# Softmax denominators of differential attention: from ones-matmuls to running sums on VectorE and GpSimd

## What is computed

```
def differential_attention(q, k, v, lam, lambda_init, subln_g):
    # q,k: (B,S,H,2,64), H=4; v: (B,S,H,128)
    s = einsum('bqhcd,bkhcd->bhcqk', q, k) * scale - slope[h] * (qpos - kpos)
    s = where(kpos <= qpos, s, -inf)
    p = softmax(s, axis=-1)                # one for each of the two components c
    a = p[:, :, 0] - lam * p[:, :, 1]
    o = einsum('bhqk,bkhv->bqhv', a, v)
    return rmsnorm(o, subln_g) * (1 - lambda_init)
```

## Time and profile before

| | us |
|---|---|
| median of 3 runs | 2340.25 |
| the three runs | 2335.2, 2340.25, 2495.3 |
| the profiled execution | 2335.61 |
| span of its slowest core (core 4) | 2334.0 |
| spans of all cores | 2320.5 to 2334.0 |
| mean granted TensorE clock of the cores | 0.928 to 0.932 of full speed |

### The profile page before, as it was taken

How to read it: one execution, slowest core, us unless ns; L and a number is a source line. 1 busy time by engine, 2 the same in 40 slices (tenths; PEclk the granted TensorE clock), 3 DMA queues, 4 the chain that set the end, 5 groups by cost and what they waited for, 6 DMA issues and landing times.

```text
span 2334.0 us, 27831 instructions; the slowest of 8 cores (2320.5 to 2334.0 us)
## 1 busy us (share of the span) xinstructions
PE 1940.9 (83%) x9248; PEld 775.1 (33%) x9248; DVE 678.2 (29%) x797; ACT 1198.8 (51%) x1754; POOL 168.3 (7%) x265
## 2 busy tenths in 40 slices
PE   2378767779999999999999886698889449999999
PEld 1133323332232233232223221343333224444444
DVE  2245445540101101111111243444442131414131
ACT  2165444538888788887888774435421120303030
POOL 1100000000000000000000111111111000000000
PEclk9699889999999999999999998798899769999999
DMA  5477886610000002000100001120100641111101
GB/s 102 81 141 144 152 144 153 146 46 1 1 1 1 1 1 73 1 1 1 45 29 1 6 26 51 40 82 8 75 37 28 224 163 43 67 54 55 55 19 63
DMA packets 45738, 137.64 MB, mean 59 GB/s; under 512 B 6144, under 2 KB 11392, under 8 KB 45216
## 3 DMA queue, kind: packets, MB, share of 16 engines
q1 hardware_dynamic: 36528, 106.28, 14.0%
q0 software_dynamic: 9072, 29.59, 8.7%
HBM read 148.66 MB, written 43.12 MB: 82 GB/s over the span
## 4 chain that ended last, share of the span: by engine, by line
PE 59%; DMA 11%; DVE 9%; ACT 9%; issue 8%; POOL 3%; ACTq 0%; DVEq 0%; POOLq 0%; SPq 0%
PE psum L152 59%; DVE arena L152 9%; ACT arena L152 9%; DMA arena<-xkv 4%; DMA arena<-w_in 4%; POOL arena L152 3%; DMA arena<-w_b 3%; DMA arena<-x1s 1%; ACTq L142 0%; DVEq L142 0%; DMA arena<-cst 0%; DMA arena<-xhalo 0%; DMA arena<-biastab 0%; SPq L152 0%; POOLq L142 0%
## 5 line engine op out<-in xcount | busy, mean ns | idle before, releaser
L152 PE MATMUL psum<-arena 128*128 128x512 bf16 (+3 forms) x9248 | 1940.9, 373 | 389.2 <-DVE arena L152 163.9
L152 PEld LDWEIGHTS psum<-arena 128*128 128x128 bf16 (+1 forms) x9248 | 775.1, 100 | 1554.5 <-issue 935.4
L152 ACT ACTIVATE arena<-psum,arena 128x1024 bf16<-128x1024 f32 (+2 forms) x872 | 765.8, 901 | 220.2 <-PE psum L152 194.4
L152 ACT ACTIVATE arena<-psum 128x512 f32<-128x512 f32 (+2 forms) x352 | 193.2, 573 | 632.9 <-PE psum L152 592.0
L152 DVE COPY arena<-psum 128x1024 bf16<-128x1024 bf16 (+1 forms) x148 | 99.9, 684 | 707.5 <-PE psum L152 707.2
L152 ACT ACTIVATE arena<-arena 128x1 f32<-128x1 f32 (+3 forms) x397 | 203.8, 519 | 194.5 <-DMA arena<-x1s 88.1
L152 DVE SCALAR_TENSOR_TENSOR arena<-arena 128x1024 bf16<-128x1024 f32 (+3 forms) x150 | 164.6, 1098 | 383.0 <-ACT arena L152 349.5
L152 POOL TENSOR_TENSOR arena<-arena 128x128 bf16<-128x128 bf16 (+3 forms) x192 | 132.2, 691 | 1138.6 <-ACT arena L152 665.3
L152 DVE SCALAR_TENSOR_TENSOR arena<-psum,arena 128x512 bf16<-128x512 f32 x208 | 147.5, 713 | 177.1 <-ACT arena L152 163.7
L152 DVE TENSOR_TENSOR arena<-psum,arena 128x512 f32<-128x512 f32 x128 | 88.2, 691 | 324.8 <-PE psum L152 247.9
L152 DVE RECIPROCAL arena<-arena 128x512 f32<-128x512 f32 x32 | 107.0, 3344 | 0.0
(11 more groups left out here) (9 smaller groups left out, 3.8 us busy)
## 6 DMA issues: line engine op xcount, KB each, us to landing
arena<-xkv SPq DMA_DIRECT2D x80, 512.0 KB, 5.4
arena<-x1s SPq DMA_DIRECT2D x32, 512.0 KB, 3.4
arena<-w_b SPq DMA_DIRECT2D x16, 1024.0 KB, 7.5
w_b<-w POOLq DMA_DIRECT2D x8, 1024.0 KB, 12.9
w_b<-w POOLq DMA_DIRECT2D x16, 512.0 KB, 7.0
x1s<-arena SPq DMA_DIRECT2D x16, 512.0 KB, 2.6
out<-arena SPq DMA_DIRECT2D x16, 512.0 KB, 2.7
wg_b<-w_in POOLq DMA_DIRECT2D x4, 1024.0 KB, 12.9
```

Of the source, the lines that this page charges most:

```text
L152: return lambda e: getattr(e, name)(*a, **k)
```

## The change

The two ones-matmuls of each tile are taken out. In their place the probabilities of a tile are added, element by element, into a float32 buffer of 128 x 1024 (`accs`): component 0 by VectorE, component 1 by GpSimd, each 512 columns (fewer in diagonal tiles). The first tile of a pass is a copy in place of an addition. There are two such buffers, used by head passes in turn. Two tiles after the last one of a pass (`finalize_part1b`) a float32 matmul of ones for each component sums the buffer over partitions into banks 6 and 7. The reciprocals read these banks directly, so VectorE's two copies are gone, and the two multiplications with them move from VectorE to GpSimd. ScalarE's copies stay where they were (`finalize_part1a`). `finalize_part2` comes eight tiles after the last one in place of six. `NPT` goes from 4 to 8.

```diff
--- before.py
+++ after.py
@@ -492,7 +492,8 @@
         ONT_END = A2.get(0)
         o_bias = A2.get(NBC * 4)
         o_tri = A2.get(256); o_ones = A2.get(256); o_onesf = A2.get(512)
-        NPT = 4
+        NPT = 8
+        o_acc = [A2.get(4096) for _ in range(2)]
         o_PT = [A2.get(2048) for _ in range(NPT)]
         o_f = [A2.get(2048) for _ in range(7)]
         onT = view(o_onT, [4, 2048], BF16)
@@ -504,6 +505,8 @@
         t_bias = Tok("bias"); t_const2 = Tok("const2")
         t_PT = [Tok("PT") for _ in range(NPT)]
         t_f = [Tok("f") for _ in range(7)]
+        accs = [view(o, [1024], F32) for o in o_acc]
+        t_acc = [[Tok("acc") for _ in range(2)] for _ in range(2)]
         P.emit("sync", I("dma_start", out=biasv, in_=biastab), writes=[t_bias], stream="ld_c")
         P.emit("pool", I("dma_start", out=tri, in_=cst[:, 128:256]), writes=[t_const2], stream="ld_cp")
         P.emit("dve", I("memset", ones, 1.0), writes=[t_const2])
@@ -563,6 +566,11 @@
                 lst[-1]["last"] = True
                 tiles += lst
         NT = len(tiles)
+        _g = -1
+        for tl_ in tiles:
+            if tl_.get("first", False):
+                _g += 1
+            tl_["grp"] = _g
         ptc = [0]
         sc = [0]
 
@@ -609,24 +617,32 @@
             pt, c0 = tl["pt"], tl["c0"]
             first = tl.get("first", False)
             last = tl.get("last", False)
+            a_ = tl["grp"] % 2
             for comp in range(2):
                 rhs = PT[pt][:, 512 * comp + c0:512 * comp + 512]
                 P.emit("pe", I("matmul", bank(4 + comp)[:, c0:512], lhsT=Vp[pos][:, t, h * 128:(h + 1) * 128], rhs=rhs,
                                start=first, stop=last), reads=[t_V[pos], t_PT[pt]], writes=[tb[4 + comp]])
+            for comp, eng in ((0, "dve"), (1, "pool")):
+                src = PT[pt][:, 512 * comp + c0:512 * comp + 512]
+                dst = accs[a_][:, 512 * comp + c0:512 * comp + 512]
+                if first:
+                    P.emit(eng, I("tensor_copy", out=dst, in_=src), reads=[t_PT[pt]], writes=[t_acc[a_][comp]])
+                else:
+                    P.emit(eng, I("tensor_tensor", out=dst, in0=dst, in1=src, op=ALU.add),
+                           reads=[t_PT[pt]], writes=[t_acc[a_][comp]])
+
+        def finalize_part1a():
+            P.emit("act", I("activation", out=fo1, in_=bank(4), func=AF.Copy), reads=[tb[4]], writes=[t_f[0]])
+            P.emit("act", I("activation", out=ft2, in_=bank(5), func=AF.Copy), reads=[tb[5]], writes=[t_f[1]])
+
+        def finalize_part1b(a_):
             for comp in range(2):
-                rhs = PT[pt][:, 512 * comp + c0:512 * comp + 512]
-                P.emit("pe", I("matmul", bank(6 + comp)[:, c0:512], lhsT=ones, rhs=rhs,
-                               start=first, stop=last), reads=[t_const2, t_PT[pt]], writes=[tb[6 + comp]])
-
-        def finalize_part1():
-            P.emit("act", I("activation", out=fo1, in_=bank(4), func=AF.Copy), reads=[tb[4]], writes=[t_f[0]])
-            P.emit("dve", I("tensor_copy", out=fz1, in_=bank(6)), reads=[tb[6]], writes=[t_f[2]])
-            P.emit("act", I("activation", out=ft2, in_=bank(5), func=AF.Copy), reads=[tb[5]], writes=[t_f[1]])
-            P.emit("dve", I("tensor_copy", out=fz2, in_=bank(7)), reads=[tb[7]], writes=[t_f[3]])
-            P.emit("dve", I("reciprocal", out=fz1, in_=fz1), reads=[t_f[2]], writes=[t_f[2]])
-            P.emit("dve", I("tensor_tensor", out=fo1, in0=fo1, in1=fz1, op=ALU.mult), reads=[t_f[2]], writes=[t_f[0]])
-            P.emit("dve", I("reciprocal", out=fz2, in_=fz2), reads=[t_f[3]], writes=[t_f[3]])
-            P.emit("dve", I("tensor_tensor", out=ft2, in0=ft2, in1=fz2, op=ALU.mult), reads=[t_f[3]], writes=[t_f[1]])
+                P.emit("pe", I("matmul", bank(6 + comp), lhsT=onesf, rhs=accs[a_][:, 512 * comp:512 * comp + 512],
+                               start=True, stop=True), reads=[t_const2, t_acc[a_][comp]], writes=[tb[6 + comp]])
+            P.emit("dve", I("reciprocal", out=fz1, in_=bank(6)), reads=[tb[6]], writes=[t_f[2]])
+            P.emit("pool", I("tensor_tensor", out=fo1, in0=fo1, in1=fz1, op=ALU.mult), reads=[t_f[2]], writes=[t_f[0]])
+            P.emit("dve", I("reciprocal", out=fz2, in_=bank(7)), reads=[tb[7]], writes=[t_f[3]])
+            P.emit("pool", I("tensor_tensor", out=ft2, in0=ft2, in1=fz2, op=ALU.mult), reads=[t_f[3]], writes=[t_f[1]])
             P.emit("dve", I("scalar_tensor_tensor", out=fo, in0=ft2, scalar=small[:, 3:4], in1=fo1, op0=ALU.mult, op1=ALU.add),
                    reads=[t_f[0], t_f[1], t_small], writes=[t_f[4]])
             P.emit("pool", I("tensor_tensor", out=fsq, in0=fo, in1=fo, op=ALU.mult), reads=[t_f[4]], writes=[t_f[5]])
@@ -657,16 +673,24 @@
             tl = tiles[i]
             emit_pv(tl)
             if tl.get("last", False):
-                finalize_part1()
-                sched.append((i + FDELAY, tl["s"], tl["h"]))
+                finalize_part1a()
+                sched.append((i + 2, "b", tl["grp"] % 2, None))
+                sched.append((i + 2 + FDELAY, "2", tl["s"], tl["h"]))
+                sched.sort(key=lambda x: x[0])
                 if tl["h"] == 3 and tl["s"] > 0:
                     load_p3a_group(3 - tl["s"])
             while sched and sched[0][0] <= i:
-                _, s_, h_ = sched.pop(0)
-                finalize_part2(s_, h_)
+                _, kind_, a1_, a2_ = sched.pop(0)
+                if kind_ == "b":
+                    finalize_part1b(a1_)
+                else:
+                    finalize_part2(a1_, a2_)
         while sched:
-            _, s_, h_ = sched.pop(0)
-            finalize_part2(s_, h_)
+            _, kind_, a1_, a2_ = sched.pop(0)
+            if kind_ == "b":
+                finalize_part1b(a1_)
+            else:
+                finalize_part2(a1_, a2_)
 
         def alias(tok, olds):
             for o in olds:
@@ -676,7 +700,7 @@
                         tok.r[ins.stream] = ins
             return tok
 
-        P2_TMP = [t_bias, t_const2] + t_PT + t_f
+        P2_TMP = [t_bias, t_const2] + t_PT + t_f + t_acc[0] + t_acc[1]
         KV03 = kv_toks([0, 1, 2, 3])
         KV47 = kv_toks([4, 5, 6, 7])
         A3 = Alloc([(kvm(0), kvm(4)), (M47_FREE, kvm(8)), (KV_END, COMMON_END), (ONT_END, ARENA_BYTES)])
```

## The result

The changed kernel took 2610.52 us in the median of nine runs (2605.89 to 2696.54) against 2342.14 for the kernel before; the ratio of the two is 1.1147, with a 95% interval of 1.113 to 1.1164. It is slower by 268 us. The forecast was slower, 2558 us, in a range of 2420 to 2760.

A forecast was written before the change was run, and what follows sets the result against it. TensorE was taken to bound the attention, and after the change VectorE and GpSimd excluding each other; 202 - 10 + 26 = 218 us on 2335.6 gave 2554, or 2558 us against the median, range 2420 to 2760.

The forecast's parts named there:

- What bounds the kernel and what the removal is worth: Attention tiles: TensorE sets 1.29 us in heads 1 to 3; removing two matmuls saves at most 69 us.
- the faster rival: Full tiles: GpSimd repeats within 1.13 us, ScalarE sets the pace, 69 us saved, near 2271 us; chance 0.06.
- GpSimd's price: GpSimd's accumulation per tile: between 1.04 and 1.27 us, repeating alone every 1.21 to 1.44 us.
- The exclusion: Full tiles: VectorE and GpSimd accumulations exclude each other, so the period is their sum, 1.49 to 1.69, taken 1.59 us.
- the rival without overlap: Full tiles: the two accumulations exclude each other without start-up overlap, period 1.96 us, 2735 us in total; chance 0.14.
- The clock: Attention tiles: TensorE, 54% busy, gets a mean clock near 0.8, lengthening the period from 1.59 to 1.64 us.
- The end of a head: Diagonal tiles 8.0 us plus net finish 4.5 us: 12.5 us a head against 10.9 before.
- The buffers: End of a head: Exps run on until eight PT buffers are full, which spares nothing, GpSimd being late.
- The sum: Whole kernel: 202 us for full tiles, less 10 for head 0, plus 26 for ends of heads, 218 us more.

The follow-up runs named there:

- The PSUM run: Changed kernel with both accumulations kept, but VectorE's running sum in PSUM banks 6 and 7, copied to SBUF at the end of a head: 2473.43 us.
- the run with four: Changed kernel with four PT buffers in place of eight: 2650.01 us, ratio 1.1321.

## Why the prediction was right, point by point

**What bounds the kernel and what the removal is worth.** TensorE's six matmuls were the bound, as read. That removing them could give at most 69 us rested on 1.13 us as ScalarE's period. That was too long: in the kernels with one sum on VectorE, Exps recorded at 1.11 us follow one another every 1.08 us, and every 1.00 us where the scores lie ready. The step was mis-sized; it had no part in the sum, but it made the gain of the faster rival smaller than it would be.

**GpSimd's price.** Bounds 1.04 and 1.27; measured 1.15 alone. The repeat of 1.21 to 1.44 holds too: 1.30. The lower bound was no like of it, though: the row of 1038 ns is the square, which reads one tile twice. The products of the new finish, f32 into f32 from two tiles, take 1.26, so the type of the output isn't what sets the two prices apart. Why they differ stays open.

**The exclusion.** The reading of three overlaps carried the forecast, and it was right, also for plain tensor_tensor, which no row had shown. The parts were 0.93 to 1.13 and 0.56, sum 1.49 to 1.69, taken 1.59, the middle, which nothing decided. Measured 1.01 and 0.55, sum 1.56. The PSUM run shows the cause, and the run with both components on VectorE shows that two engines were worse than one. (Two slips of arithmetic change nothing: 1.11 us for GpSimd gives a period of 1.54 by the same steps, and the rival without overlap is 2736 us.)

**The clock.** This step failed, although its mean came out: 0.83 over the stage, where I expected 0.8 from busier stretches of other stages, and spread it evenly, 0.05 us a tile, 29 us. In full tiles the granted clock is 1.00 at 37.55 of 65 us busy, 58%. It is 0.50 from 723 to 739 us, around the end of a head, and 0.70 from 725 to 760. The level of 1.2 GHz thus struck in the diagonal tiles and the finish, where it made the first float32 matmul longer (1.92 us, from 737.49 on, where one at full clock took 1.10), and not in the full tiles. Stretches of similar busy share with other rhythms were no guide. What brings the fall is not shown: TensorE's wait of 7.97 us for a mask lies there (718.9 to 726.9), but in the run without masks, where its longest wait in the same stretch is 2.6 us, the clock is 0.50 there too:

```profile
723.00:739.00 16.00, 10.21 (x25) 2.52 (x24) 13.93 (x12) 6.38 (x9) 12.70 (x11) 0.50 0.00 1
```

**The end of a head.** 12.5 us forecast, 18.5 measured: the term that was mis-sized, 16 x 6 = 96 us too little. The diagonal tiles are hardly to blame, the finish is. The finish of one head in the changed kernel:

```profile
736.52 0.60 POOL L152 CAST arena<-arena 128x512 f32<-128x512 bf16 x1
...
739.51 6.57 DVE L152 RECIPROCAL arena<-psum 128x512 f32<-128x512 f32 x2 [3.22 <-PE psum L152]
...
743.07 1.26 POOL L152 TENSOR_TENSOR arena<-arena 128x512 f32<-128x512 f32 x1 [4.65 <-ACT arena L152]
...
747.65 0.75 DVE L152 SCALAR_TENSOR_TENSOR arena<-arena 128x512 f32<-128x512 f32 x1 [1.57 <-POOL arena L152]
...
748.61 1.29 POOL L152 TENSOR_TENSOR arena<-arena 128x512 f32<-128x512 f32 x1 [1.06 <-DVE arena L152]
```

From the end of GpSimd's last accumulation (736.6) to the end of its square (748.61 + 1.29) it is 13.3 us, where the sum had 7.8. The reciprocals begin 2.9 us in, not 1.0: TensorE still has matmuls of the next head to do, and the float32 matmul takes nearly 2 us at the lower clock. And there are two of them in a row, 6.57 us, where the sum had 3.34 because "the first component's part is earlier and hidden". It isn't: both matmuls stand in TensorE's queue behind the next head's first two tiles, and by then the diagonal tiles have eaten TensorE's lead, so both components come at once. The run without reciprocals confirms it with 5.0 us for two. 13.3 less the two accumulations of the next head that GpSimd does meanwhile (two periods, 3.1) is 10.2 for the finish, against 4.5; 18.5 less 10.2 leaves 8.3 for the diagonal tiles, against 8.0.

**The buffers.** "Exp work runs on under this until eight PT buffers are full, which spares nothing" was wrong by 2.3 us a head, as the run with four shows.

**The sum.** Period too long by 0.08 us (46 us too much, 29 of it the clock), end of a head too short by 6.0 (96 us too little). That the two errors partly cancelled, 2558 against 2610, is luck; that the kernel is slower because two engines exclude each other is not.

## What to carry to other kernels

Before giving one tile's work to VectorE and GpSimd in parallel, look for places in the trace where both already run, and see whether one of them is lengthened; with two SBUF inputs on VectorE here a pair took 1.56 us, most of the sum of 0.69 and 1.15, and one engine alone was faster. If both must run, VectorE's running sum in PSUM brought the period down to 1.30 us here. And price the end of a loop as a chain through the queues, not as work: what stands "earlier" in one queue is only hidden if its producer still has a lead there.

## What the runs showed that I had not expected

- The largest gain lay outside the change. Emitting the norm's sum of squares four tiles later, with nothing else, took the kernel before from 2339.71 to about 2296 us. TensorE, its bound, had waited in each of 16 heads for GpSimd's square: its idle time before float32 matmuls falls from 43.1 us to 12.0, which is 31 of the 42 us.
- TensorE's granted clock stayed at 1.00 while it was busy for only 58% of the time, in short regular pauses of 0.63 us.
- ScalarE's Exps overlap: recorded length 1.11 us, period down to 1.00.
- A reciprocal of 512 columns takes 3.33 us out of PSUM and 3.34 out of SBUF, almost five times an addition; two of them are a third of the end of a head.
